# A half spectrum for the Fourier layer, and the first weight sums of a layer started before its mean is known

## What is computed

```
SUBS = ["mla", "ffn", "fourier", "ffn", "ffn", "mix", "ffn", "ffn", "mix", "ffn"]
```

```
def fourier_mixer(h, w_f):
    hg = h.astype(jnp.float32).reshape(B, T, FOURIER_GROUPS, FOURIER_GROUP_DIM)
    f = jnp.fft.fft2(hg, axes=(1, 3), norm="ortho").real
    return f.reshape(B, T, D_MODEL).astype(h.dtype) @ w_f

def layer_norm(x, g, b):
    mu = jnp.mean(x32, axis=-1, keepdims=True)
    var = jnp.mean(jnp.square(x32 - mu), axis=-1, keepdims=True)
    y = (x32 - mu) * lax.rsqrt(var + LN_EPS)
    return (y * g + b)

def modulate(h, mod, j):
    return h * (1 + mod[:, j, 1][:, None, :]) + mod[:, j, 0][:, None, :]
```

## Time and profile before

| | us |
|---|---|
| median of 3 executions (2172.44 to 2174.23) | 2172.55 |
| the profiled execution | 2175.36 |
| its span | 2173.6 |
| PE busy | 2114.6 (97%) |
| DVE busy | 1256.2 (58%) |
| ACT busy | 410.0 (19%) |
| POOL busy | 494.3 (23%) |
| mean granted clock of PE | 0.984 of full speed |

### The profile page before, as it was taken

One profiled execution on the slowest core, in us unless ns is written; L12 is line 12 of the kernel. 1 busy time (PEld: TensorE's weight loads), 2 busy tenths in 40 slices (PEclk: granted clock), 3 DMA queues, 4 the chain that ended last, 5 costly groups with the idle time before them and its releaser, 6 DMA issues.

```text
span 2173.6 us, 23955 instructions
## 1 busy us (share of the span) xinstructions
PE 2114.6 (97%) x9428; PEld 1691.1 (78%) x9428; DVE 1256.2 (58%) x2465; ACT 410.0 (19%) x781; POOL 494.3 (23%) x411
## 2 busy tenths in 40 slices
PE   7999999989999999999999999999999999999996
PEld 4777888668885888688688888678867868888865
DVE  6545577654677366746433477767775643346543
ACT  3334211022110111023140211021102223121101
POOL 0100244311444144400000044414440000003340
PEclk9999999999999999999999999999999999999998
DMA  9673565874667665743434375766564343435331
GB/s 367 242 261 100 201 261 233 292 258 160 249 241 267 222 251 205 270 167 134 155 116 148 137 284 229 256 237 248 236 231 186 136 155 117 155 116 194 145 133 71
DMA packets 61551, 438.37 MB, mean 202 GB/s; under 512 B 6976, under 2 KB 8768, under 8 KB 40320
## 3 DMA queue, kind: packets, MB, share of 16 engines
q1 hardware_dynamic: 28608, 318.35, 38.3%
q0 software_dynamic: 32256, 117.45, 15.3%
q10 hardware_dynamic: 576, 1.05, 0.1%
HBM read 434.72 MB, written 2.10 MB: 201 GB/s over the span
## 4 chain that ended last, share of the span: by engine, by line
PE 94%; DVE 2%; DMA 2%; ACT 1%; issue 1%; POOL 0%; SPq 0%; ACTq 0%; DVEq 0%; POOLq 0%
PE lin L1771 27%; PE small_ps L1898 17%; PE lin L1898 13%; PE small_ps L1960 7%; PE lin L1960 6%; PE lin L1993 5%; PE small_ps L1771 4%; PE lin L2206 3%; PE pstat L1875 1%; DMA ada_ring<-in_ada 1%; PE lin L2149 1%; PE small_ps L2225 1%; PE lin L1839 1%; PE lin L2103 1%; PE small_ps L1875 1%; PE small_ps L2116 1%
## 5 line engine op out<-in xcount | busy, mean ns | idle before, releaser
L1771 PE MATMUL lin<-h,ring 128*128 128x256 f32 x1968 | 436.1, 383 | 8.0 <-ACT h L961 2.8
L1771 PEld LDWEIGHTS lin<-h,ring 128*128 128x128 f32 x1968 | 375.4, 192 | 64.4 <-issue 8.9
L588 POOL TENSOR_TENSOR proj<-ring 128x1024 f32<-128x1024 f32 x54 | 127.2, 2355 | 870.8 <-PE small_ps L1771 726.3
L1045 DVE CUSTOM_DVE_ANT_0 ada_ring<-ada_ring,crow 128x1024 f32<-128x1024 f32 x224 | 266.6, 1221 | 49.7 <-DMA ada_ring<-in_ada 49.2
L575 POOL DMA_DIRECT2D ada_ring<-in_ada x224 | 121.3, 542 | 719.0 <-DVE sums L1045 683.3
L1898 PE MATMUL small_ps<-ring,h 128*128 128x256 f32 x864 | 195.3, 379 | 0.0
L1898 PEld LDWEIGHTS small_ps<-ring,h 128*128 128x128 f32 x864 | 164.1, 190 | 22.3
L1771 PE MATMUL lin<-rec,ring 128*128 128x257 f32 (+1 forms) x608 | 147.7, 395 | 8.1 <-ACT rec L686 8.1
L1898 PE MATMUL lin<-proj,sq 128*128 128x256 f32 x672 | 153.9, 379 | 0.0
L1771 PEld LDWEIGHTS lin<-rec,ring 128*128 128x128 f32 x608 | 120.5, 199 | 28.6 <-issue 10.0
L1898 PEld LDWEIGHTS lin<-proj,sq 128*128 128x128 f32 x672 | 127.7, 190 | 17.4
(11 more groups left out here) (409 smaller groups left out, 3029.6 us busy)
## 6 DMA issues: line engine op xcount, KB each, us to landing
ring<-in_w SPq DMA_DIRECT2D x66, 2048.0 KB, 8.9
ada_ring<-in_ada POOLq DMA_DIRECT2D x224, 512.0 KB, 5.1
ring<-in_w2a SPq DMA_DIRECT2D x30, 1536.0 KB, 7.7
ring<-in_gates SPq DMA_DIRECT2D x12, 2048.0 KB, 8.3
ring<-in_w2d SPq DMA_DIRECT2D x12, 1408.0 KB, 8.0
ring<-in_mproj SPq DMA_DIRECT2D x8, 2048.0 KB, 8.1
ring<-in_mtok SPq DMA_DIRECT2D x4, 2048.0 KB, 8.4
ring<-in_branch SPq DMA_DIRECT2D x4, 2048.0 KB, 7.8
```

The costliest lines, as they stand in the source:

```text
L588: W(combined_weights(j, 0), b12, b11, ALU.subtract).then_inc(s_weights_combined, 1)
L1045: V.tensor_tensor_reduce(w, w, crow[:, 0 if s < FIRST2 else 1], 1.0, 0.0, ALU.mult, ALU.add, sums[:, s % 3, b:b + 1]).then_inc(s_ada_used, 1)
L1771: ins = mm(dst, w[:, lo:lo + m], rhs(k), start=k == 0, stop=k == nk - 1)
```

## The change

It has three parts.

**Layers 5 to 9, uncentred first units.** ACT folds `x` itself, not `xc`, and does so as soon as each tile of the residual update is in. `fold` gets a second extra column, the gain, so each raw tile sum has 258 columns and also gives the sum of gain times weight. The sum for the mean stands on PE behind the first half of the first raw unit, the sum of the squares behind the first half of the second. DVE keeps minus the mean in `minus_mean`, and `raw_scaled` becomes three steps: two copies of 2 columns, two instructions that add minus mean times the summed gain to the bank, two multiplications by `rstd`. In the ffn layers `next_tiles` leaves DVE: ACT does it after the third silu (`s_base_made`).

**Later first weight sums.** POOL's first `combine` of a folded ffn layer waits for `scaled_tiles` as well.

**Layer 2, half spectrum.** The first transform keeps 129 frequencies of cosine and of sine, 258 columns and not 512. The second makes the even part (129 columns) and the odd part (127) for tokens 0 to 128, each from 2 matmuls per half group; ACT copies the even part to `h`, and DVE makes the tokens 1 to 127 and 129 to 255 as sum and difference. The features of every second tile come out mirrored, so the rows of `w_f` are mirrored on the host. The 18 ada blocks are spread: 5 ahead, 4 between the sums and differences, 9 between the residual updates.

```diff
-ADA_IN_FOURIER = 18
+ADA_IN_FOURIER = 5
+ADA_IN_SPECTRUM = [1, 1, 0, 2]
+ADA_IN_WF = [2, 2, 2, 1, 1, 1, 0, 0]
+FREQ = T // 2 + 1
+ODD = FREQ - 2
...
@@ combine (POOL)
                     pool.wait_ge(s_unit, ph.unit0 + 2)
+                    if folded(ph.name[0]):
+                        pool.wait_ge(s_x_scaled, tiles_scaled(ph.name[0]))
...
@@ fold_in (ACT)
+                if s < len(subs):
+                    for k in range(KD):
+                        act.wait_ge(*taken(before - (KD - 1) + k))
+                        A(fold[:, k, 0:T], x[:, k], ACT.Copy, scale=fold_gain[:, k:k + 1]).then_inc(s_folded, 1)
+                        if not centred and k % 2:
+                            A(sq[:, k - 1:k + 1], x[:, k - 1:k + 1], ACT.Square).then_inc(s_fold_squares, 1)
+                if centred:
+                    for k in range(0, KD, 2):
                         act.wait_ge(s_x_centred, nth(act, s_x_centred))
                         A(sq[:, k:k + 2], xc[:, k:k + 2], ACT.Square).then_inc(s_fold_squares, 1)
...
@@ ffn units (ACT)
+                            if n == 2 and s > FIRST2:
+                                for k in range(KD):
+                                    A(x[:, k], xc[:, k], ACT.Identity, scale=next_gain[:, k:k + 1],
+                                      bias=next_shift[:, k:k + 1]).then_inc(s_base_made, 1)
...
@@ raw_scaled (DVE), layers 5 to 9
+                    for c in range(2):
+                        V.tensor_copy(raw_columns(r, c), banks[c][:, T:T + 2]).then_inc(s_dve_chain, 1)
+                    for c in range(2):
+                        dve.wait_ge(s_dve_chain, nth(dve, s_dve_chain))
+                        V.scalar_tensor_tensor(dst[:, c], minus_mean, raw_gain(r, c), banks[c][:, 0:T],
+                                               ALU.mult, ALU.add).then_inc(s_dve_chain, 1)
+                    for c in range(2):
+                        dve.wait_ge(s_dve_chain, nth(dve, s_dve_chain))
+                        ins = V.tensor_tensor(dst[:, c], dst[:, c], rstd[:], ALU.mult)
...
@@ residual (DVE)
+                    if name == "wf":
+                        ada(ADA_IN_WF[m])
...
@@ Fourier layer (DVE)
+                    for n in range(4):
+                        dve.wait_ge(s_even_kept, nth(dve, s_even_kept))
+                        for j in range(2):
+                            even = h[:, 2 * n + j, 1:1 + ODD]
+                            odd = lin[(u + n) % NBANK][:, j * T + FREQ:(j + 1) * T]
+                            mirror = h[:, 2 * n + j, T - 1:T - 1 - ODD:-1]
...
+                        ins.then_inc(s_taken_by_dve, 1)
+                        ada(ADA_IN_SPECTRUM[n])
...
@@ fourier (PE)
-                        for n, (tt, c) in enumerate(((0, 0), (0, 1), (1, 0), (1, 1))):
-                            ins = mm(b[:, j * T:(j + 1) * T], fa[:, 2 * g + tt, c * T + j * P:c * T + j * P + P],
-                                     dft_t[:, tt, c], start=n == 0, stop=n == 3)
+                        for c, (lo, hi) in enumerate(((0, FREQ), (FREQ, T))):
+                            for tt in range(TT):
+                                at = c * FREQ + j
+                                ins = mm(b[:, j * T + lo:j * T + hi], spectrum(2 * g + tt)[:, at:at + P],
+                                         dft_t[:, tt, lo:hi], start=tt == 0, stop=tt == TT - 1)
```

More of the change, by code:

```diff
@@ L306, in phase @@
             unit0[s, name] = len(takes)
-            for _ in range(units):
-                count[taker] += 1
-                takes.append((taker, count[taker]))
+            for who in taker if isinstance(taker, tuple) else (taker,) * units:
+                count[who] += 1
+                takes.append((who, count[who]))
         nf = nm = 0
@@ L1012, in _ @@
                     for n in range(8):
[L1013 removed]
+                        take(u + n, [(spectrum(n), 0, 2 * FREQ, 0, P)])
                     for n in range(4):
[L1015 removed]
+                        act.wait_ge(s_unit, u + 8 + n + 1)
+                        if n == 0:
+                            act.wait_ge(s_unit, u + 8)
+                        even = lin[(u + 8 + n) % NBANK][:].rearrange("p (a b) -> p a b", a=2)[:, :, 0:FREQ]
+                        A(h[:, 2 * n:2 * n + 2, 0:FREQ], even, ACT.Copy).then_inc(s_even_kept, 1)
                 if kind == "mix":
@@ L1244, in next_tiles, with raw_scaled @@
                         V.tensor_scalar(x[:, k], xc[:, k], next_gain[:, k:k + 1], next_shift[:, k:k + 1], ALU.mult, ALU.add)
-            def raw_scaled(u, r, dst):
+            def raw_scaled(s, u, r, dst):
                 dve.wait_ge(s_unit, u + 1)
                 banks = (lin[u % NBANK], second_bank[r])
[L1250 to L1253, removed]
+                if s < FIRST2:
+                    for c in range(2):
+                        V.tensor_copy(raw_shift(r, c), banks[c][:, T:T + 1])
+                    for c in range(2):
+                        ins = V.tensor_tensor(dst[:, c], banks[c][:, 0:T], rstd[:], ALU.mult)
+                else:
+                    for c in range(2):
+                        V.tensor_copy(raw_columns(r, c), banks[c][:, T:T + 2]).then_inc(s_dve_chain, 1)
+                    for c in range(2):
+                        dve.wait_ge(s_dve_chain, nth(dve, s_dve_chain))
+                        V.scalar_tensor_tensor(dst[:, c], minus_mean, raw_gain(r, c), banks[c][:, 0:T],
+                                               ALU.mult, ALU.add).then_inc(s_dve_chain, 1)
+                    for c in range(2):
+                        dve.wait_ge(s_dve_chain, nth(dve, s_dve_chain))
+                        ins = V.tensor_tensor(dst[:, c], dst[:, c], rstd[:], ALU.mult)
                 ins.then_inc(s_raw_scaled, 1)
@@ L1679, in _ @@
                     u0 = unit0[s, FIRST_PHASE[kind]]
-                    raw_scaled(u0, 0, raw_pair(0) if kind == "ffn" else proj[:, QI:QI + 2])
+                    raw_scaled(s, u0, 0, raw_pair(0) if kind == "ffn" else proj[:, QI:QI + 2])
                     scaled_tiles(s)
                     if kind == "mix":
-                        raw_scaled(u0 + 1, 1, proj[:, QI + 2:QI + 4])
+                        raw_scaled(s, u0 + 1, 1, proj[:, QI + 2:QI + 4])
                         next_tiles(s)
@@ L1800, in folded_squares_summed, with mean_summed @@
                 ins.then_inc(s_sums_over_features, 1)
+            def mean_summed():
+                pe.wait_ge(s_tiles_added, nth(pe, s_tiles_added, KD - 1))
+                mm(pa[2][:, 0:T], ones[:], rstd[:], start=True, stop=True).then_inc(s_mean_sums, 1)
             def raw_unit(ph, r):
@@ L2382, in _ @@
                     project(s, "wout", merged_tile)
-                if s >= FIRST2:
-                    pe.wait_ge(s_tiles_added, nth(pe, s_tiles_added, KD - 1))
-                    mm(pa[2][:, 0:T], ones[:], rstd[:], start=True, stop=True).then_inc(s_mean_sums, 1)
+            mean_summed()
             folded_squares_summed()
```

92 lines of the change are left out of this document (57 added, 35 removed).

## The result

| | before | after |
|---|---|---|
| median us (executions) | 2173.24 (4, 2172.44 to 2174.23) | 2149.12 (4, 2145.16 to 2150.09) |
| the profiled execution, us | 2175.36 | 2148.71 |
| its span, us | 2173.6 | 2146.9 |
| mean granted clock of PE | 0.984 | 0.988 |

The ratio is 0.9885, with a 95% interval of 0.9868 to 0.9903: 25.0 us less, between 21.1 and 28.7. The forecast was 2148.

What follows compares the result with a forecast made beforehand. PE is busy 97% of the span, so only omitted matmuls or PE's waits give time. Layers 5 to 9 give 24.4 - 10.8 = 13.6 us, Fourier 11.1: 24.7 off 2175.36 is 2150.7, as median 2148; range 2133 to 2158.

Steps and rivals of the forecast that it cites:

- the step itself: Into layers 5 to 9, PE goes on without a gap: 4.9 us for each of five steps, 24.4 us gained.
- What POOL's sums give back: Layers 6, 7, 9: POOL's sums delay DVE's multiplications, PE waits 1.9 us for the combination of h; 10.8 us lost.
- The prediction's second witness: Layer 6: eight DVE instructions for x took 4.69 us beside POOL, cited as showing that SBUF operands are held up.
- the 1.7 us for the clock: Behind PE's waits at the combination in layers 6, 7, 9, a lowered clock costs 1.7 us more each.
- near 0.6 behind it: Sign: PE's granted clock near 0.6 behind its wait for DVE's combination of h in layers 6, 7 and 9.
- Fourier: Layer 2: shorter transforms, `w_f` 14.7 us earlier, but PE waits 5 us for update 3, plus 1.7 clock; gain 11.1 us.
- The bound of 19.3 us: Fourier layer: largest possible gain, 19.3 us, if ada blocks are not starved and `w_f` runs through.
- A: Rival, ffn layers: DVE keeps up, its multiplications not held by POOL; gain 24.4 + 11.1, 2137 us; chance 0.2.
- B: Rival: A, and the Fourier layer's ada blocks don't hold PE either; 2129 us; chance 0.05.
- C: Rival, Fourier's second transform: 128-column matmuls bound by weight loads, costing 14 us as before; 2151 us; chance 0.05.
- D: Rival, ffn layers: DVE enters the nine pairs late, stays late; 27 pairs wait, 46 us, 2194 us; chance 0.03.
- E: Rival, ffn layers: PE also waits for the fourth unit's banks or product, about 3 us more each; 2157; chance 0.12.

Runs made afterwards that it cites:

- Run 3: Changed kernel with DVE's mean addition written back to PSUM, so multiplications (and the ffn product) read one operand there: 2139.93 us, 0.9959 of the changed kernel.
- run 1: Changed kernel with the Fourier layer as it was, so only the parts of layers 5 to 9: 2157.62 us, ratio 0.9929 to the kernel before.
- run 5: Changed kernel with layer 3's second 2 MB weight load delayed until 16 of 18 ada blocks are used: 2139.73 us, 0.9964 of the changed kernel.
- run 6: Changed kernel with 13 instead of 18 ada blocks in the Fourier layer, five moved to layer 3: 2138.46 us, 0.9954 of the changed kernel.
- run 7: Changed kernel with the edits of Run 3 and run 6 together: 2132.58 us, ratio 0.9816 to the kernel before, 0.9930 of the changed kernel.
- run 4: Changed kernel without POOL's wait for the scaled tiles before its first weight sums: 2148.42 us, ratio 0.9887 to the kernel before.
- run 8: Changed kernel with the first addition of DVE's combination of h written three times in layers 6, 7 and 9: 2156.59 us, 1.0046 of the changed kernel.
- run 2: Kernel before with the Fourier part alone (half spectrum and spread ada blocks): 2163.51 us, ratio 0.9956 to the kernel before.

## Why the prediction was right

Forecast 2148, measured 2149.12. That is closer than its terms were; two errors of some 4 and 3 us pull in opposite directions, which is luck. The two large terms, by its own steps:

**Layers 5 to 9, the step itself: right.** 4.9 us per step were expected. The mix layers, which give nothing back, lost 4.6 and 4.8 us, and the path into the second half unit is 3.92 us long for 3.9. Into layer 5 this is 4.65 us less, of which 2.75 are the two waits and 1.7 the clock behind them (5.16 us for 3.49): it was low in all five steps before and in none now.

**What POOL's sums give back: the mechanism right, the size too large.** The forecast, from the last matmul on (1205.97 in layer 6): scaled tiles at 18.6, the held unit's end at 24.4, the combination's at 31.0, PE there at 29.1. Measured 18.5, 23.9, 30.4 and 29.2. The wait was therefore 1.6 us and not 1.9, in the three layers named. Run 3 shows its cause, since only the place of the operands differs. The Trainium skill (SBUF — State Buffer, Who interferes with whom) has the rule that a DVE instruction with two SBUF inputs contends with a GpSimd instruction that reads SBUF, while one with at most one such input, outside the modes that use both ports, does not; the 4.11 us beside POOL and the 0.42 us with a PSUM operand agree with it. The prediction's second witness, the row of 4.69 us, is of another kind: those eight instructions read one SBUF tile each. They were held as well, since eight take 2.67 us in layer 5 without POOL, but they say nothing of a second input. **The term that was mis-sized is the 1.7 us for the clock behind each of these waits.** The first 16 recorded instructions behind each of the three run in 3.69 us, and the clock there is 1.00; the sign "near 0.6 behind it" did not come. I had taken the price from a place in which PE waits twice, as the timeline of the kernel before has it at the start of layer 5:

```profile
940.31 0.67 PE L2385 MATMUL small_ps<-rstd,ones 128*128 128x256 f32 x2 [1.20 <-DVE rstd L1314]
942.54 5.16 PE L1771 MATMUL lin<-rec,ring 128*128 128x257 f32 x16 [1.55 <-ACT rec L686]
```

That is 2.75 us of idle time within 3.4 us, and I carried its price to a single wait of 1.6. The 10.8 us given back were 4.8. The net gain of these layers was 17.8 us in the profile and not 13.6. By the times alone that would not be shown: the interval of run 1, 12.6 to 18.2 us, takes in both.

**Fourier: the mechanism right, most steps close.** The first transform ends 9.36 us after its start with the copy's wait (forecast 8.7 and 0.5), the second takes 7.4 us for 7.2. With the later start taken off, `w_f` begins at 462.8 for 462.6, update 3 is done at 489.4 for 489.9, and layer 3 begins at 498.7 for 498.5. Update 2 was expected near 481 and done at 477.8, and PE came to unit 6 at 483.7 for 484.6. The wait was 5.8 us for 5, the clock cost 2.4 for 1.7. Runs 5 and 6 take it away from two sides, so the cause is shown: blocks starved by the 2 MB load, and updates queued behind them. The bound of 19.3 us "with no starving" is what both reach: 63.44 - 44.25 = 19.2.

**The sum** came near because its errors cancel in part: 17.8 and 10.9 us for 13.6 and 11.1, less 2.6 us for the later start and for layers 3 and 4, for which it had no term and of which at least the start is chance. The 0.6 us that are then missing from the 26.7 of the span I have not placed.

**The rivals.** A (no wait at the combination) did not come; run 3 makes it by its edit, at 2140 for 2137. B is run 7, at 2133, for 2129. C is refuted: 64 recorded instructions of 129 and 127 columns, with new weights for each, take 7.41 us, 0.116 each, where 64 of 256 columns took 14.08. The rule that the prediction names beside C does not hold here. Of D there is no sign: no wait for `first_gate`. Of E one form appears in run 4, where the fourth unit's banks make PE wait 1.1 us a layer; the wait at the combination shrank by 0.4 us a layer in exchange, so it added 0.7.

## What to carry to other kernels

- When work is moved under an engine that was idle, look at what the gap had covered: here a shorter path on PE uncovered DVE beside POOL. Whether a multiplication on DVE reads one tile from PSUM or both from SBUF decided there whether it took 0.42 us or waited for POOL.
- Work with slack should not stand in the same queue ahead of work that is waited for, least of all where its transfer can be starved by a large load: moving five blocks to a later layer gave back 8.3 us of the Fourier stretch here.
- Price the clock as a risk, not as a fixed fee: behind one and the same wait of 2.76 us it was low in some executions and not in others. A difference of a few us between two kernels can come from that alone.

## What the runs showed of the hardware

- **The clock behind a single wait.** Behind the waits of 1.1 to 1.7 us at the start of layers 6, 7 and 9 (changed kernel, runs 1, 4, 5 and 6) the next 16 recorded instructions always ran at full speed, in 3.69 or 3.73 us. Behind the 1.74 us in the Fourier layer of run 1 it stayed at 1.00. Behind the wait of 1.93 us at the first matmul on `h` in layer 4 the clock was low in six of the ten profiles (a mean of 0.96 over the window from 700 to 740 that holds it, and 1.00 in the other four). Behind the 2.76 us at the start of the program it was low in six of ten, behind the 3.0 us of run 8 in one place of three. Behind the 2.64 us in the Fourier layer of the kernel before it was 0.66. Behind the 3.63 us ahead of the Fourier layer it was low in the changed kernel as well (0.57 from 447.5 to 451.5), and there the first transform takes 8.89 us or more in every kernel with the half spectrum. Behind 5.78 us it was 0.50. What decides between equal waits stays open.
- **A transfer of 0.5 MB beside one of 2 MB** took 11.38 us from issue to landing, against 4.76 alone; on the Fourier chains of runs 1 to 4 and 8 such landings take 9.6 to 11.2 us.
- **PSUM as destination and operand** of one DVE multiplication beside POOL's sum: 0.42 us, no longer than with an SBUF destination.
